# Output projection of a hybrid decoder block: 512-column products for its first half, a last quarter token tile by token tile

## What is computed

```python
y = merged @ w_out[l]            # (512, 1024) @ (1024, 1024)
x = x + y                        # residual
out = x * rsqrt(mean(x*x, -1) + RMS_EPS) * final_g
```

## Time and profile before

| | |
|---|---|
| median of 3 runs | 485.36 us (483.79 to 490.91) |
| the profiled execution | 488.13 us, of which 486.3 us from first to last instruction (the span) |
| PE busy | 445.1 us (92%) |
| DVE, ACT, POOL busy | 301.5, 186.3, 155.1 us |
| chain that ended last | PE 79%, DVE 7%, DMA 5%, ACT 4% |
| output projection on PE | 430.44 to 476.7 us |
| from PE's last product to the end of the span | 9.6 us |
| mean granted clock of PE | 0.971 of full speed |

### The profile page before, as it was taken

How to read it: one execution, slowest core, us unless ns; L and a number is a source line. 1 busy time by engine, 2 the same in 40 slices (tenths; PEclk the granted TensorE clock), 3 DMA queues, 4 the chain that set the end, 5 groups by cost and what they waited for, 6 DMA issues and landing times.

```text
span 486.3 us, 7294 instructions
## 1 busy us (share of the span) xinstructions
PE 445.1 (92%) x2811; PEld 360.1 (74%) x2811; DVE 301.5 (62%) x670; ACT 186.3 (38%) x370; POOL 155.1 (32%) x78
## 2 busy tenths in 40 slices
PE   0999999989879999989989979999999999999992
PEld 0788887889457886555656557888888888899991
DVE  2679899899989958978897871107134152072234
ACT  5733433064023335795555441222222222243323
POOL 0414444031033300242313132435444444344420
PEclk9989999999979999989999988999999999999997
DMA  8933530941872017501011010393334333332104
GB/s 248 292 91 83 177 87 1 147 123 43 246 186 45 0 20 215 116 1 44 1 44 42 4 45 5 83 337 94 88 86 116 102 88 86 108 105 92 45 0 173
DMA packets 68450, 47.53 MB, mean 98 GB/s; under 512 B 12760, under 2 KB 65440, under 8 KB 68256
## 3 DMA queue, kind: packets, MB, share of 16 engines
q1 hardware_dynamic: 67232, 47.00, 35.6%
q10 hardware_dynamic: 1184, 0.07, 0.2%
HBM read 42.87 MB, written 4.19 MB: 97 GB/s over the span
## 4 chain that ended last, share of the span: by engine, by line
PE 79%; DVE 7%; DMA 5%; ACT 4%; issue 3%; SPq 1%; DVEq 0%; ACTq 0%
PE bank L811 21%; PE bank L812 20%; PE bank L813 20%; PE bank L1037 3%; PE bank L1076 3%; PE bank L1055 3%; DMA raw<-in_w_in 2%; PE bank L955 2%; PE bank L926 1%; PE bank L1017 1%; DMA x_sb<-in_x 1%; DVE prob L1476 1%; DVE z L1155 1%; PE bank L860 1%; DMA raw<-in_cmp_w_v 1%
## 5 line engine op out<-in xcount | busy, mean ns | idle before, releaser
L588 POOL TENSOR_TENSOR w_lo<-raw,w_hi 128x1024 fp32r<-128x1024 f32 (+2 forms) x57 | 138.0, 2421 | 270.1 <-ACT w_hi L616 270.1
L811 PE MATMUL bank<-hT_lo,w_hi 128*128 128x512 f32 x288 | 116.8, 405 | 0.1
L812 PE MATMUL bank<-hT_hi,w_lo 128*128 128x512 f32 x288 | 114.7, 398 | 0.0
L813 PE MATMUL bank<-hT_hi,w_hi 128*128 128x512 f32 x288 | 114.4, 397 | 0.0
L616 ACT ACTIVATE w_hi<-raw 128x1024 fp32r<-128x1024 f32 (+2 forms) x57 | 59.5, 1044 | 84.0 <-PE bank L813 68.3
L811 PEld LDWEIGHTS bank<-hT_lo,w_hi 128*128 128x128 f32 x288 | 55.4, 192 | 13.5 <-issue 1.6
L813 PEld LDWEIGHTS bank<-hT_hi,w_hi 128*128 128x128 f32 x288 | 55.5, 193 | 12.0
L812 PEld LDWEIGHTS bank<-hT_hi,w_lo 128*128 128x128 f32 x288 | 55.5, 193 | 11.0
L762 ACT ACTIVATE prob<-prob,nmax 128x128 f32<-128x128 f32 (+2 forms) x64 | 35.3, 552 | 25.2 <-DVE nmax L1476 25.1
L812 PE MATMUL bank<-w_hi,m_lo 128*128 128x256 f32 x128 | 36.2, 283 | 0.0
L813 PE MATMUL bank<-w_hi,m_hi 128*128 128x256 f32 x128 | 36.2, 283 | 0.0
(11 more groups left out here) (207 smaller groups left out, 757.4 us busy)
## 6 DMA issues: line engine op xcount, KB each, us to landing
raw<-in_w_in SPq DMA_DIRECT2D x32, 512.0 KB, 3.8
raw<-in_w_out SPq DMA_DIRECT2D x8, 512.0 KB, 3.4
x_sb<-in_x SPq DMA_DIRECT2D x4, 512.0 KB, 5.6
raw<-in_cmp_w_k SPq DMA_DIRECT2D x4, 512.0 KB, 3.8
raw<-in_cmp_w_v SPq DMA_DIRECT2D x4, 512.0 KB, 4.3
raw<-in_w_in SPq DMA_DIRECT2D x8, 256.0 KB, 3.8
raw<-in_w_proj_s SPq DMA_DIRECT2D x4, 512.0 KB, 3.4
raw<-in_w_proj_nsa SPq DMA_DIRECT2D x8, 256.0 KB, 4.0
```

The lines of the kernel that those rows point to most:

```text
L588: nc.gpsimd.tensor_tensor(view(w_lo, j % NSPLIT, dims), w, view(w_hi, j % NSPLIT, dims).bitcast(F32), ALU.subtract).then_inc(lo_done, 1)
L811: nc.tensor.matmul(dst, w[0], x[1], start=first, stop=False, skip_group_check=True)
L812: nc.tensor.matmul(dst, w[1], x[0], start=False, stop=False, skip_group_check=True)
L813: return nc.tensor.matmul(dst, w[0], x[0], start=False, stop=last, skip_group_check=True)
```

## The change

The first half of the output columns is now made in blocks `wa0` to `wa3`: two channel tiles by 512 columns each, the same 512 KB. For each of them PE goes over the four token tiles, each with a whole bank: 24 products of 512 columns for a block, 96 in place of 192. The third quarter stays as it was. For the last quarter PE first waits for both blocks, `wo3_0` and `wo3_1`, and then finishes one token tile after the other: 24 products of 256 columns for a tile. The split of `wo3_1` goes into the room of `f_hi` and `f_lo`, which nothing else uses by then. Residual, squares, sum, root and scaling are done by tile in the last quarter; both engines scale each tile, DVE its columns 0 to 511 and ACT its columns 512 to 1023; and SP stores each half by itself.

```diff
-    b += [(f"wo{q}_{h}", 1) for q in range(4) for h in range(2)]
+    b += [(f"wa{n}", 1) for n in range(4)]
+    b += [(f"wo{q}_{h}", 1) for q in (2, 3) for h in range(2)]
...
+        def split_views(name):
+
+            dims = wdims(name)
+            if name == "wo3_1":
+                return [f[:, 0:2, :].rearrange("p a t -> p (a t)").rearrange("p (k n) -> p k n", n=dims[1]) for f in (f_hi, f_lo)]
+            return [view(w, slot(name), dims) for w in (w_hi, w_lo)]
...
-                sp.dma_start(out[0, P * i:P * i + P, :], r_sb[:, i, :]).then_inc(stored, 16)
-            sp.wait_ge(stored, 16 * NT)
+                sp.dma_start(out[0, P * i:P * i + P, 0:512], r_sb[:, i, 0:512]).then_inc(stored, 16)
+                sp.wait_ge(y_high_ready[i], 1)
+                sp.dma_start(out[0, P * i:P * i + P, 512:1024], r_sb[:, i, 512:1024]).then_inc(stored, 16)
+            sp.wait_ge(stored, 2 * 16 * NT)
...
+                if name == "wo3_1":
+                    wait_fill(ac, "B7")
+                elif j >= NSPLIT:
                     wait_used(ac, split_names[j - NSPLIT])
...
+            def square(n, i, cols):
+                junk = (qr, z)[n % 2][:, i, 0:cols.stop - cols.start]
+                nc.scalar.activation(junk, r_sb[:, i, cols], ACT.Square, accum_out=ssq4[:, i, n:n + 1]).then_inc(fin_sq, 1)
+
+            for n in range(4):
+                after(f"wa{n}")
+            for i in range(NT):
+                ac.wait_ge(r_done, i + 1)
+                square(0, i, slice(0, 512))
+            after("wo2_0")
+            after("wo2_1")
+            for i in range(NT):
+                ac.wait_ge(r_done, NT + 1 + i // 2)
+                square(1, i, slice(512, 768))
+            for i in range(NT):
+                ac.wait_ge(r_done, NT + 3 + i)
+                square(2, i, slice(768, 1024))
+                ac.wait_ge(fin_var, i + 1)
+                nc.scalar.activation(rms[:, 2, i:i + 1], rms[:, 1, i:i + 1], ACT.Sqrt).then_inc(fin_sqrt, 1)
+                ac.wait_ge(root_done, i + 1)
+                nc.scalar.activation(r_sb[:, i, 512:1024], r_sb[:, i, 512:1024], ACT.Copy, scale=rms[:, 3, i:i + 1])\
+                    .then_inc(y_high_ready[i], 1)
...
+            def merged(kt, i):
+                return [v[:, kt, P * i:P * i + P] for v in (m_hi, m_lo)]
+
+            for n in range(4):
+                w = weights(f"wa{n}")
+                for i in range(NT):
+                    if n == 0:
+                        open_bank(pe, f"WA{i}")
+                    for kk in range(2):
+                        kt = 2 * n + kk
+                        if i == 0:
+                            pe.wait_ge(m_split, kt + 1)
+                        ins = mm3(bk(f"WA{i}")[:, :], merged(kt, i), [v[:, kk, :] for v in w], kt == 0, kt == KT - 1)
+                    if n == 3:
+                        fill(ins, f"WA{i}")
+                if n < 3:
+                    ins.then_inc(part_used, 1)
+
+            for h in range(2):
+                w = weights(f"wo2_{h}")
+                for m in range(2):
+                    job = f"W2_{m}"
                     if h == 0:
-                        ins.then_inc(part_used, 1)
+                        open_bank(pe, job)
+                    for ii in range(2):
+                        for kk in range(4):
+                            kt = 4 * h + kk
+                            ins = mm3(bk(job)[:, 256 * ii:256 * ii + 256], merged(kt, 2 * m + ii), [v[:, kk, :] for v in w],
+                                      kt == 0 and ii == 0, kt == KT - 1)
+                    if h == 1:
+                        fill(ins, job)
+                if h == 0:
+                    ins.then_inc(part_used, 1)
+
+            w = weights("wo3_0"), weights("wo3_1")
+            pe.wait_ge(r_done, NT)
+            for i in range(NT):
+                open_bank(pe, f"W3_{i}")
+                for kt in range(KT):
+                    ins = mm3(bk(f"W3_{i}")[:, 0:256], merged(kt, i), [v[:, kt % 4, :] for v in w[kt // 4]], kt == 0, kt == KT - 1)
+                fill(ins, f"W3_{i}")
...
+                residual(f"WA{i}", slice(i, i + 1), slice(0, 512))
             for m in range(2):
-                two = slice(2 * m, 2 * m + 2)
-                ve.wait_ge(fin_sq, 12 + 2 * (m + 1))
-                link(V.tensor_reduce(rms[:, 0, two], ssq4[:, two, :], AX_X, ALU.add))
-                variance(fin_var, two.start, two.stop)
-                times_gain(3, two)
-                inverse_root(fin_sqrt, m + 1, two.start, two.stop, root_done)
-                if m == 0:
-                    residual(3, 1)
-                i = 2 * m
-                ve.wait_ge(rg_done, 4 + m)
-                V.tensor_scalar(r_sb[:, i, :], r_sb[:, i, :], rms[:, 3, i:i + 1], None, MUL).then_inc(y_ready[i], 1)
+                ve.wait_ge(fin_sq, 2 * m + 2)
+                times_gain(slice(2 * m, 2 * m + 2), slice(0, 512))
+            for m in range(2):
+                residual(f"W2_{m}", slice(2 * m, 2 * m + 2), slice(512, 768))
+            ve.wait_ge(fin_sq, 2 * NT)
+            times_gain(slice(0, NT), slice(512, 768))
+
+            for i in range(NT):
+                residual(f"W3_{i}", slice(i, i + 1), slice(768, 1024))
+                ve.wait_ge(fin_sq, 2 * NT + i + 1)
+                link(V.tensor_reduce(rms[:, 0, i:i + 1], ssq4[:, i:i + 1, 0:3], AX_X, ALU.add))
+                variance(fin_var, i, i + 1)
+                times_gain(slice(i, i + 1), slice(768, 1024))
+                ve.wait_ge(rg_done, 4 + i)
+                inverse_root(fin_sqrt, i + 1, i, i + 1, root_done)
+                V.tensor_scalar(r_sb[:, i, 0:512], r_sb[:, i, 0:512], rms[:, 3, i:i + 1], None, MUL).then_inc(y_ready[i], 1)
```

More of the change, by code:

```diff
@@ L191, in bank_plan @@
                 pj(f"{kind}{d}")
-    for q in range(4):
-        for m in range(2):
-            pj(f"W{q}_{m}")
+    for i in range(NT):
+        pj(f"WA{i}", 0)
+    for m in range(2):
+        pj(f"W2_{m}")
+    for i in range(NT):
+        pj(f"W3_{i}")
     return jobs
@@ L355, in build_program @@
             "final_sqrt", "times_gain", "final_root", "stored"))
-        y_ready = [sem(f"out{i}_ready") for i in range(NT)]
+        y_ready = [sem(f"out{i}_low_ready") for i in range(NT)]
+        y_high_ready = [sem(f"out{i}_high_ready") for i in range(NT)]
         zhi_done, fhi_done = sem("z_hi_done"), sem("f_hi_done")
@@ L817, in weights @@
                 pe.wait_ge(lo_done, split_at[name] + 1)
-                dims = wdims(name)
-                return [view(w, slot(name), dims) for w in (w_hi, w_lo)]
+                return split_views(name)
             def hT(kt, cols=slice(0, T)):
@@ L1114, in _ @@
                     channel_major(f"MA{d}", f"mga{d}")
-            for q in range(4):
-                for h in range(2):
-                    w = weights(f"wo{q}_{h}")
-                    for m in range(2):
-                        job = f"W{q}_{m}"
-                        if h == 0:
-                            open_bank(pe, job)
-                        for ii in range(2):
-                            i = 2 * m + ii
-                            for kk in range(4):
-                                kt = 4 * h + kk
-                                pe.wait_ge(m_split, kt + 1) if q == 0 and m == 0 and ii == 0 else None
-                                x = [v[:, kt, P * i:P * i + P] for v in (m_hi, m_lo)]
-                                ins = mm3(bk(job)[:, 256 * ii:256 * ii + 256], x, [v[:, kk, :] for v in w],
-                                          kt == 0 and ii == 0, kt == KT - 1)
-                        if h == 1:
-                            fill(ins, job)
-                    if h == 0:
-                        ins.then_inc(part_used, 1)
+            def merged(kt, i):
+                return [v[:, kt, P * i:P * i + P] for v in (m_hi, m_lo)]
@@ L1548, in _, with residual @@
             ve.wait_ge(gfin_in, 16)
-            def residual(q, m):
-                job = f"W{q}_{m}"
+            def residual(job, tiles, cols):
                 wait_fill(ve, job)
-                r2 = r_sb[:, 2 * m:2 * m + 2, 256 * q:256 * q + 256]
-                V.scalar_tensor_tensor(out=r2, in0=bk(job)[:, :].rearrange("p (i c) -> p i c", i=2), scalar=0.125,
+                n, width = tiles.stop - tiles.start, cols.stop - cols.start
+                r2 = r_sb[:, tiles, cols]
+                V.scalar_tensor_tensor(out=r2, in0=bk(job)[:, 0:n * width].rearrange("p (i c) -> p i c", i=n), scalar=0.125,
@@ L1555, in residual @@
                                        in1=r2, op0=MUL, op1=ADD).then_inc(r_done, 1)
-            def times_gain(q, tiles):
-                r = r_sb[:, tiles, 256 * q:256 * q + 256]
-                n = tiles.stop - tiles.start
-                V.tensor_tensor(r, r, gfin[:, 256 * q:256 * q + 256].unsqueeze(1).broadcast_to((P, n, 256)), MUL)\
-                 .then_inc(rg_done, 1)
-            for q in range(3):
-                for m in range(2):
```

(20 more changed lines are left out.)

39 lines of the change are left out of this document (15 added, 24 removed).

## The result

The changed kernel takes 484.07 us in the median (480.55 to 488.48, 20 runs), against 487.79 us for the kernel before in the same comparison (483.79 to 491.74, 20 runs). The medians lie 3.7 us apart. The ratio is 0.9935, with a 95% interval of 0.9905 to 0.9964, which is 3.2 us less. The forecast said 3.4 us less, and 482.0 us for the new median. That absolute number is 2.1 us too low, and 484.07 lies above the forecast's own range of 480.6 to 483.2 (inside the wide one of 480.0 to 485.0). The base explains it: the median before was 485.36 in three runs and is 487.79 in twenty.

What follows compares the result with a forecast made beforehand. PE, busy 445.1 of 486.3 us, and an uncovered 9.6 us tail bound it. PE 1.3 less 0.6, plus 1.3 from the tail, and uncrowded stores made 3.4 less: 485.36 to 482.0 us; own range 480.6 to 483.2, wide 480.0 to 485.0.

Steps and rivals of the forecast that it cites:

- The wider products: First half on PE: 96 products of 512 columns replace 192 of 256, each pair 13.3 ns less, saving 1.3 us.
- The supply keeps up: First half: weights are split 3.78 us after their buffer's release, within a block's 5.44 us, so waiting costs nothing.
- The new wait: Entry to the last quarter: PE waits for both weight blocks, released by POOL's low part at 464.2; loses 0.6 us.
- The gain without POOL: Third quarter's gain on DVE: takes 1.22 us in place of 1.92, as POOL no longer runs beside it.
- The tile chain: Last quarter: DVE needs 3.09 us from tile to tile against PE's 2.88, so DVE sets the pace.
- ACT's scaling: Last quarter: ACT's scaling of 512 columns takes about 0.65 us, so ACT keeps up.
- The stores: End of the span: tiles' stores come 3.09 us apart, uncrowded; last half issued at 480.2 lands at 482.5.
- The rival of 3.8 us: Last stores: still land 3.8 us after issue, span only 1.9 us less, 483.5 us; chance 0.12.
- The sum: Whole change: span from 486.3 to 482.9, 3.4 us less; on the median 485.36 this gives 482.0 us.
- wide products for nothing: Rival, first half: 512-column products run at 0.2374 us, gaining 0.25 us in place of 1.3; 483.0 us; chance 0.05.
- a chain of 3.5 us: Rival, last quarter: 3.5 us between residuals, last scaling 1.2 later, 483.2 us; chance 0.12 together with the long stall.
- The clock rival: Last quarter: PE's standstill lowers its clock, about 0.10 us more per 256-column product, up to 9.6 us, 491.6; chance 0.02.

Runs made afterwards that it cites:

- e1: Against the kernel before, only the first half gets 512-column products; the last quarter stays in pairs: 54.57 us from first output-projection product to span end, against 55.86.
- e4: Changed kernel with `wo3_0` split early into the spare room, `wo3_1` into `wo2_0`'s buffer: 51.89 us from first output-projection product to span end, against 52.77.
- e9: Changed kernel with DVE scaling a tile's low half behind the next tile's residual: 52.24 us from first output-projection product to span end, against 52.77.
- e8_best: Changed kernel with `wo3_0` split early, low-half scaling behind the next residual, last high half stored by ACT: ratio 0.9924 to the kernel before, 483.48 us.

## Why the prediction was right, point by point

- **The wider products, 1.3 us.** Right: 1.29 in the e1 kernel, 0.2267 each in the trace after.
- **The supply keeps up.** Right: there is no gap between 426.03 and 459.18. (The last `m_lo` is needed at 447.4 on the forecast's scale and not at 446.8, one product group into the fourth block; nothing hangs on it.)
- **The new wait, 0.6 us.** The mechanism is right: POOL's low part of `wo3_1` releases PE, as said. The size was 0.78. The step that missed is "ACT starts at 458.21", 0.25 behind the release: after, ACT starts the split 0.53 behind it. Of these 0.28 us, 0.12 was made good behind it, since POOL's two low parts overlap by 0.06 where the forecast set them 0.06 apart; POOL's instructions, 2.42 and 2.40 for 2.39, took a little back. The e4 kernel shows that the gap costs its full length.
- **The gain without POOL, 1.22 us.** Right: 1.23, and 1.93 with POOL beside it in the e1 kernel.
- **The tile chain, 3.09 us on DVE.** Right: 3.08; residual to scaling 465.91 - 463.23 = 2.68 for 2.70. The e9 kernel shows that the chain binds and not PE.
- **ACT's scaling, 0.65 us.** Mis-sized: 0.72. The line through 256 and 1024 columns came from a square (0.40) and a scaling (1.15), which are not the same instruction; from 0.72 and 1.15 a scaling of 256 columns would be some 0.5, by estimate. It cost nothing at the end, since ACT was done 0.18 us before SP issued the last half.
- **The stores.** The path is right: the last half is issued behind SP's issue of the one before it, and lands 2.3 us later, as forecast (480.2 to 482.5). The term that was a little short is the distance of the two issues, 0.38 in place of 0.3: 0.33 of issue and 0.05 to the next. The rival of 3.8 us is gone.
- **The sum.** Stage 52.46 forecast, 52.77 measured, 0.31 more. The last scaling starts 0.13 later than forecast (48.96 against 49.09): PE's gap gave 0.19, and the tiles' chain took 0.06 of it back. From there to the issue of the last half it is 0.10 more, and 0.08 more from its landing to the end, a landing that is shown to 0.1 us only.
- **The rivals.** Stores at 3.8 us, wide products for nothing, a chain of 3.5 us: none showed. (The 0.2374 us of the second one stands in no row; the product took 0.2267.) The clock rival did not come at 0.78 us, but its mechanism is real: at 3.83 us the clock fell, and one product of 256 columns then cost 93 ns more, where 0.10 us was forecast. Its 1.5 us came from 16 products, and not 96, which makes it much cheaper than its worst case of 9.6 us.

The forecast put all of the 3.4 us in the last 56 us of the span and used the trace's own products, hand-overs and landing times. That is why it held: each term was the difference of two rows that the new kernel still has. The same forecast set against the two profiled spans (7.5 us apart) would have looked wrong by 4.1 us: the 4.4 us that stand ahead of the stage, where the clock was low for 17 us less, less the 0.3 of the sum above.

The difference was right by its mechanism; the number 482.0 was not. It hung on the median of three runs, which twenty runs put 2.4 us higher. Only the wider range, drawn from the spread of those three runs, held the 484.07.

## What to carry to other kernels

At the end of a kernel, compare stages that start at a fixed instruction; spans of single executions differ by more than such a change brings (483.79 to 491.74 us for one kernel). Take the base of an absolute forecast from more than three runs. Cutting the tail to one tile paid here, until the chain on one engine (3.08 us) was longer than PE's tile (2.88). Then reorder that engine, so that its scaling fills the wait for another's square. Where PE is made to wait for two weight blocks at once, the last of them should have been split before; here 0.9 us lay in that order alone, and a stall of 3.8 us cost 1.5 us more through the clock in the one execution that was profiled.

## What the runs showed of the hardware

- A float32 product of 128 columns with weights of its own takes 111.5 ns, one of 256 takes 120 and one of 512 takes 226.7, all at full clock. Halving 256 columns gains 8.5 ns of 120.
- The clock's fall is seen late: after a standstill of 3.83 us PE ran at full clock for 1.15 us and then at half for 3.4 us, while it was busy.
- The length of a standstill does not decide alone. One of 3.16 to 3.17 us, at the same place of the program, was followed by the lower clock in eight kernels and by the full one in two; one of 2.2 us near 210 us by the lower clock in nine and by the full one in one (after). Ahead of the output projection the clock was low for 20 us and more in seven of the ten profiled executions, and for 3 to 14 us in the others.
- The exclusion between DVE and POOL works both ways: a gain of 1.23 us took 1.93 behind POOL, and a low part of 2.40 us took 3.51 behind DVE's gains. With POOL's start 0.02 us apart, both orders occurred (e4_early_split and e8_best).
- ACT can start an instruction 0.32 us after its wait has ended, in place of 0.04, with no cause that the profile shows (the split of `wo3_0`, in six kernels).
- In the kernel after, a store of 256 KB lands 2.0 to 2.7 us after its issue on SP (medians 2.1 for the first half of a tile and 2.3 for the second, issued 0.38 us behind it). The one from ACT, 0.24 behind SP's, took 2.5. Stores of 512 KB some 3.1 us apart take 2.6 in the median. The last whole store was issued at 49.89 us and the last half at 49.99, and the half still ends 0.18 earlier.
